# Two of the four weight sums of each group made by accumulating DMAs

## Chip, core and metric

One core of one Trainium2 chip. The metric is device time in microseconds (us) of one launch; a few runs are taken and their median counts. The hardware profiler also records one execution, and every row below is from that one.

## What is computed

The reference is one layer of a hybrid model for 512 prompt tokens and 8 decoded tokens (T = 520 columns). The change lies in its last three products, which are 2048 wide on the input side:

```python
def _channel_and_ple(h, mix, p_l, w_out, g_ffn, w_up, w_down, w_ple, w_ple_norm, w_ple_gate):
    h = h + mix @ w_out
    u = _rmsnorm(h, g_ffn)
    h = h + jnp.square(jax.nn.relu(u @ w_up)) @ w_down
    e = _rmsnorm(p_l @ w_ple, w_ple_norm) * jax.nn.sigmoid(h @ w_ple_gate)
    return h + e
```

## The kernel before

The products with `w_up`, `w_down` and `w_ple_gate` run in 72 groups `g` (32, 32 and 8). One group makes 256 output rows for all 520 columns out of a 2048 x 256 piece of the weights. The group uses a two-by-two scheme with seven products instead of eight (Strassen's scheme in Winograd's form): the piece is cut into four blocks W11, W12, W21, W22 of 1024 x 128, the activations into four as well, and four sums of weight blocks (T1 to T4) and four of activation blocks enter the seven products. In this text the seven products are numbered 0 to 6, their weights being W11, T2, W21, T3, T1, T4 and W22.

A weight is used in two parts of reduced width, high and low: ScalarE (ACT) writes the high part (`w_high`, line 1145, tile `wh`), VectorE (DVE) subtracts it from the weight and writes the low part (`w_low`, line 2460, tile `wl`). TensorE (PE) then does 24 matmuls of 260 columns: 16 with the high weights (lines 1893 and 1895) and 8 with the low ones (line 1900). `wh` and `wl` have two buffers each, so the high part of product n+2 waits for the high matmuls of product n.

The blocks land in six SBUF buffers `rb` of 512 KB each. The sums overwrite blocks that are no longer needed, and a buffer is free for the next load when its last reader is done:

```python
b22 = lambda g: g % 2
b12 = lambda g: 2 + g % 2
b11 = lambda g: 3 - g % 2
B_T, B21 = 4, 5
```

All four sums are DVE instructions: T3 = W22 - W12 into buffer 4 (`sum_t3`, line 2439), T1 = W12 - W11 over W12 (`sum_t1`, line 2444), T2 = W11 + T3 over W11 (`sum_t2`, line 2449) and T4 = W21 - T2 over W21 (`sum_t4`, line 2454). T4 of group g stands on DVE behind the low part of product 2, T3 of group g+1 behind the low part of product 4, T1 of g+1 behind that of product 6, T2 of g+1 behind that of the next group's product 0. The order on each engine is written out by hand: `vector_group` (DVE) and `act_group` (ACT) walk through the seven steps `i` of a group, and the low or high part made in step i is that of product i+1. SyncE (SP) issues nearly all DMAs from one queue in program order and waits before each for its buffer: `block12(g+1)`, `block11(g+1)`, `block21(g+1)`, then the store of hidden rows (in the first 32 groups), then `block22(g+2)`.

Beside this DVE adds the seven products in PSUM up to the four output blocks (lines 2507, 2632, 2642, 2636, `add_first`, `add_second`), makes the activation sums, and every eight groups in `w_down` the whole set of seven activation operands is changed ("a turn"): SP loads operands of 1040 KB each (line 730, tile `af`), ACT and DVE split them (lines 1198 and 2430). GpSimd (POOL) has next to nothing in groups 0 to 63 and adds squares for the last norm in groups 64 to 71 (lines 1401, 1402).

Of the kernel before, what the change touches and what calls it, by code (L numbers as in the profile page):

```python
# [23 lines left out]
P = 128  # L24
# [75 lines left out]
def build(nc, d, d_out):  # L100
    ctx = ExitStack()
    with ctx:
# [349 lines left out]
        t_sum, T_SUM0 = a_b, 64  # L452
        w_lo, W_LO0 = a_nm, 32
# [3 lines left out]
        r_sq, R_SQ0 = d_v, 5  # L457
# [3 lines left out]
        x_i, X_I0 = e_sc, 8  # L461
# [67 lines left out]
        def _(sp):  # L529
# [189 lines left out]
            def operand(c, i):  # L719
# [10 lines left out]
                sp.dma_start(af[n % 9], o_scr[c, SLOT[i]]).then_inc(op_in[n % 4], 16)  # L730
# [28 lines left out]
            for g in range(GN):  # L759
# [8 lines left out]
                if g + 1 < GN:  # L768
                    block12(g + 1)
# [44 lines left out]
        def _(act):  # L814
# [309 lines left out]
            def w_high(w):  # L1124
# [8 lines left out]
                elif i == 1:  # L1133
                    act.wait_ge(t_sum, T_SUM0 + 4 * g + 3)
                elif i == 2:
                    act.wait_ge(b_in[B21], B_IN0[B21] + 16 * (g + 1))
                elif i == 3:
                    act.wait_ge(t_sum, T_SUM0 + 4 * g + 1)
                elif i == 4:
                    act.wait_ge(t_sum, T_SUM0 + 4 * g + 2)  # L1140
# [52 lines left out]
            def operand_high(phase, i, half):  # L1193
                n = 7 * phase + i
                if half == 0:
                    act.wait_ge(op_in[n % 4], OP_IN0[n % 4] + 16 * landings(n))
# [118 lines left out]
        def _(pool):  # L1315
# [95 lines left out]
            pool.wait_ge(h_fin, H_FIN0 + 8)  # L1411
            step(pool.memset(acc, 0.0))  # L1412
            for j in range(8):
                add_squares(16 + j, 0, None, sqg, acc)
# [554 lines left out]
        def _(dve):  # L1969
# [829 lines left out]
```

## Time and profile before

| | |
|---|---|
| median of 3 runs | 2766.38 us (2764.25 to 6148.04) |
| the profiled execution, its own time | 2768.17 us |
| its span in the trace | 2766.4 us |
| granted TensorE clock, mean | 0.955 |
| PE busy | 2527.4 us (91%) |
| DVE busy | 2032.5 us (73%) |
| ACT busy | 1167.5 us (42%) |
| POOL busy | 516.5 us (19%) |
| first and last high matmul of the 72 groups (line 1893) start at | 1184.6 and 2739.1 us |

The 72 groups are 56% of the span. The part ahead of them (input projection, attention, state space part, output projection) is not touched by the change. In the rows below, a line of a view of waits says who waited for whom, how long in all, how often, and the longest; a line of the timeline has the start, the duration, the engine and the line, and in brackets the idle time ahead of it with its releaser.

### The profile page before, as it was taken

What the parts mean: (1) busy time and instruction counts of PE and PEld (TensorE: products, weight loads), DVE (VectorE), ACT (ScalarE), POOL (GpSimd) and SP (SyncE); (2) the same over time, 40 slices, a digit from 0 to 9 for tenths busy, and PEclk for the clock granted to TensorE, in tenths of its full rate; (3) what the DMA queues carried; (4) which work ended last, traced back from release to release, by engine and by line L of the source; (5) the groups of instructions that cost most, each with busy time, mean ns of one, the idle gap of its engine ahead of it and who ended that gap; (6) DMA issues with size and microseconds to landing.
All of it is one profiled execution on the core that took longest, in us unless ns stands there. A gap on an engine that the chain in (4) does not pass through costs nothing. (4 is left out here: it accounts for less than half of the span.)

```text
span 2766.4 us, 50293 instructions
## 1 busy us (share of the span) xinstructions
PE 2527.4 (91%) x20031; PEld 2395.9 (87%) x20031; DVE 2032.5 (73%) x2475; ACT 1167.5 (42%) x1675; POOL 516.5 (19%) x258
## 2 busy tenths in 40 slices
PE   7999999967785899789999999999989999998897
PEld 7999999942354899779999999999989999898897
DVE  4277877627658522698887888888888888889997
ACT  3111111127653322355665665563444434433543
POOL 0099899500018010310000000000000000000022
PEclk9999999988876999899999999999999999999898
DMA  4388898579922332345655656575665646643343
GB/s 134 89 281 272 272 294 297 169 265 389 354 93 84 124 103 97 123 121 163 176 156 163 176 156 179 176 225 162 195 208 179 224 145 192 199 131 100 93 127 126
DMA packets 487361, 498.71 MB, mean 180 GB/s; under 512 B 17270, under 2 KB 434676, under 8 KB 481847
## 3 DMA queue, kind: packets, MB, share of 16 engines
q1 hardware_dynamic: 464136, 482.48, 54.6%
q10 hardware_dynamic: 22990, 13.01, 1.6%
q8 instruction: 159, 2.61, 0.4%
q14 instruction: 76, 0.61, 0.1%
HBM read 428.83 MB, written 66.70 MB: 179 GB/s over the span
## 5 line engine op out<-in xcount | busy, mean ns | idle before, releaser
L1893 PE MATMUL ps<-ah,wh 128*128 128x260 f32 x4032 | 1001.4, 286 | 57.9 <-DVE xsc L2642 13.8
L1895 PE MATMUL ps<-al,wh 128*128 128x260 f32 x4032 | 995.1, 284 | 0.0
L1893 PEld LDWEIGHTS ps<-ah,wh 128*128 128x128 f32 x4032 | 767.9, 190 | 67.5 <-issue 19.4
L1145 ACT ACTIVATE wh<-rb 128x1024 fp32r<-128x1024 f32 x504 | 532.4, 1059 | 671.7 <-PE ps L1895 454.1
L1895 PEld LDWEIGHTS ps<-al,wh 128*128 128x128 f32 x4032 | 768.5, 191 | 0.1
L2460 DVE TENSOR_TENSOR wl<-rb,wh 128x1024 fp32r<-128x1024 f32 x504 | 619.8, 1230 | 100.4 <-ACT wh L1145 97.8
L1900 PE MATMUL ps<-ah,wl 128*128 128x260 f32 x4032 | 576.2, 285 | 16.3 <-DVE wl L2460 15.8
L1900 PEld LDWEIGHTS ps<-ah,wl 128*128 128x128 f32 x4032 | 525.5, 191 | 19.8 <-DVE wl L2460 19.6
L1468 PE MATMUL ps<-uh,wh 128*128 128x260 f32 x1952 | 517.4, 286 | 18.3 <-DVE wl L1978 14.8
L1470 PE MATMUL ps<-ul,wh 128*128 128x260 f32 x1952 | 513.9, 284 | 0.0
L1978 DVE TENSOR_TENSOR wl<-raw,wh 128x1024 fp32r<-128x1024 f32 (+1 forms) x130 | 215.9, 1662 | 258.2 <-ACT wh L839 257.6
L1473 PE MATMUL ps<-uh,wl 128*128 128x260 f32 x1952 | 394.6, 284 | 0.0
L1468 PEld LDWEIGHTS ps<-uh,wh 128*128 128x128 f32 x1952 | 372.2, 191 | 19.8 <-DVE wl L1978 11.3
L1341 POOL TENSOR_TENSOR kpage<-kpage,qbc 128x1024 f32<-128x1024 f32 x128 | 353.9, 2799 | 164.0 <-DMA kpage<-in_cache_k 163.9
L1470 PEld LDWEIGHTS ps<-ul,wh 128*128 128x128 f32 x1952 | 371.4, 190 | 0.0
L839 ACT ACTIVATE wh<-raw 128x1024 fp32r<-128x1024 f32 (+1 forms) x130 | 134.3, 1035 | 561.4 <-PE ps L1473 504.6
L1473 PEld LDWEIGHTS ps<-uh,wl 128*128 128x128 f32 x1952 | 303.4, 190 | 0.0
L1412 POOL MEMSET acc<- 128x520 f32 x1 | 0.5, 532 | 1373.5 <-DVE hT L2555 1373.5
L2045 DVE TENSOR_REDUCE sc<-kpage 128x16 f32<-128x1024 f32 x128 | 154.1, 1212 | 71.8 <-POOL kpage L1341 71.8
L1568 PE MATMUL ps<-vpage,zpad 128*32 128x512 f32 x512 | 78.4, 740 | 32.3 <-DMA vpage<-in_cache_v 32.2
L2444 DVE TENSOR_TENSOR rb<-rb,rb 128x1024 f32<-128x1024 f32 x72 | 95.4, 1325 | 8.2 <-DMA rb<-in_w_down 7.7
L2439 DVE TENSOR_TENSOR rb<-rb,rb 128x1024 f32<-128x1024 f32 x72 | 88.9, 1235 | 16.9 <-issue 15.5
(403 smaller groups left out, 2232.3 us busy)
## 6 DMA issues: line engine op xcount, KB each, us to landing
kpage<-in_cache_k SPq DMA_DIRECT2D x128, 512.0 KB, 4.9
vpage<-in_cache_v SPq DMA_DIRECT2D x128, 512.0 KB, 5.8
rb<-in_w_up SPq DMA_DIRECT2D x128, 512.0 KB, 4.0
rb<-in_w_down SPq DMA_DIRECT2D x128, 512.0 KB, 4.1
raw<-in_w_in SPq DMA_DIRECT2D x88, 512.0 KB, 4.6
af<-o_scr SPq DMA_DIRECT2D x28, 1040.0 KB, 9.9
raw<-in_w_out SPq DMA_DIRECT2D x32, 512.0 KB, 3.4
rb<-in_w_ple_gate SPq DMA_DIRECT2D x32, 512.0 KB, 4.0
```

Source lines behind the costliest of these rows:

```text
L839: A(wh[:, c % 2, 0:elems], raw[:, c % 2, 0:elems], ACT.Copy).then_inc(hi_ready, 1)
L1145: A(wh3[:, w % 2], w_source(g, i), ACT.Copy).then_inc(w_hi, 1)
L1341: pool.tensor_tensor(kpage[:, s], kpage[:, s], qbc[:, b], ALU.mult).then_inc(s_km, 1)
L1468: mm(ps[:, bank + 2 * m + f, 0:HALF], h_, xh[:, f * HALF:(f + 1) * HALF], start=st, stop=False)
L1470: mm(ps[:, bank + 2 * m + f, 0:HALF], h_, xl[:, f * HALF:(f + 1) * HALF], start=False, stop=False)
L1473: z = mm(ps[:, bank + 2 * m + f, 0:HALF], l_, xh[:, f * HALF:(f + 1) * HALF], start=False, stop=en)
L1893: mm(out, wh3[:, w % 2, k], ah[n][:, k], start=fresh and k == 0, stop=False, skip_group_check=True)
L1895: last = mm(out, wh3[:, w % 2, k], al[n][:, k], start=False, stop=False, skip_group_check=True)
L1900: last = mm(out, wl3[:, w % 2, k], ah[n][:, k], start=False, stop=k == KP - 1, skip_group_check=True)
L1978: tt(wl[:, c % 2, 0:elems], raw[:, c % 2, 0:elems], wh[:, c % 2, 0:elems].bitcast(F32), ALU.subtract).then_inc(lo_ready, 1)
L2045: dve.tensor_reduce(sc[:, pg // PAGES, pg % PAGES, :], kpage[:, pg % 4].rearrange("p (c n) -> p c n", n=DK), AX, ALU.add)\
L2460: tt(wl3[:, w % 2], w_source(w // 7, w % 7), wh3[:, w % 2].bitcast(F32), ALU.subtract).then_inc(w_lo, 1)
```

## The change

T3 and T4 are no longer DVE instructions. GpSimd issues for each a DMA from one `rb` buffer to another that adds what it reads to what lies there. Such a DMA can only add, so signs are turned: T3 = W22 + W12, T1 = W12 + W11, T2 = W11 + T3, T4 = W21 + T2, and the signs come back in the activation sums and in the output sums. For T3 the target buffer 4 must first hold W12, so SP loads that block a second time (`block12_again`). T3 of group 0 stays on DVE. One output add over 520 columns (`add_first`) becomes two over 260, as one now adds and the other subtracts. POOL's adding of squares moves into the same loop as its DMAs. Several semaphores are re-used for others, and the landing semaphores of the operands become five instead of four.

```diff
             def block12(g):
                 if g >= 1:
-                    sp.wait_ge(t_sum, T_SUM0 + 4 * (g - 1) + 4)
+                    sp.wait_ge(t4_acc, 16 * g)
                 block(g, b12(g), 0, 1)
+
+            def block12_again(g):
+                sp.wait_ge(w_lo, W_LO0 + 7 * (g - 1) + 4)
+                sp.dma_start(rb[B_T], w_block(g, 0, 1)).then_inc(bt_in, 16)
...
                 if g + 1 < GN:
+                    block12_again(g + 1)
                     block12(g + 1)
...
                 elif i == 3:
-                    act.wait_ge(t_sum, T_SUM0 + 4 * g + 1)
+                    act.wait_ge(t_sum, T_SUM0 + 1)
+                    if g:
+                        act.wait_ge(t3_acc, 16 * g)
...
                 elif i == 5:
-                    act.wait_ge(t_sum, T_SUM0 + 4 * g + 4)
+                    act.wait_ge(t4_acc, 16 * (g + 1))
...
+            def accumulate_t4(g):
+                pool.wait_ge(t_sum, T2_AT(g))
+                pool.wait_ge(w_lo, W_LO0 + 7 * g + 3)
+                pool.dma_start(rb[B21], rb[b11(g)], accum_op=ALU.add).then_inc(t4_acc, 16)
+
+            def accumulate_t3(g):
+                pool.wait_ge(bt_in, BT_IN0 + 16 * g)
+                pool.wait_ge(b_in[b22(g)], B_IN0[b22(g)] + 16 * (g // 2 + 1))
+                pool.dma_start(rb[B_T], rb[b22(g)], accum_op=ALU.add).then_inc(t3_acc, 16)
+
+            for g in range(GN):
+                accumulate_t4(g)
+                if g + 1 < GN:
+                    accumulate_t3(g + 1)
+                if g == GG:
+                    pool.wait_ge(h_fin, H_FIN0 + 8)
+                    step(pool.memset(acc, 0.0))
+                if g > GG:
+                    add_squares(16 + g - GG - 1, 0, None, sqg, acc)
+            add_squares(23, 0, None, sqg, acc)
...
             def sum_t2(g):
-                dve.wait_ge(t_sum, T_SUM0 + 4 * g + 2)
+                dve.wait_ge(b_in[b11(g)], B_IN0[b11(g)] + 16 * (g + 1))
+                dve.wait_ge(t_sum, T1_AT(g))
+                if g:
+                    dve.wait_ge(t3_acc, 16 * g)
                 dve.wait_ge(w_lo, W_LO0 + 7 * g + 1)
                 tt(rb[b11(g)], rb[b11(g)], rb[B_T], ALU.add).then_inc(t_sum, 1)
-
-            def sum_t4(g):
-                dve.wait_ge(t_sum, T_SUM0 + 4 * g + 3)
-                dve.wait_ge(w_lo, W_LO0 + 7 * g + 3)
-                tt(rb[B21], rb[B21], rb[b11(g)], ALU.subtract).then_inc(t_sum, 1)
...
-                tt(both, both, X2.unsqueeze(1).to_broadcast([P, 2, HALF]), ALU.add).then_inc(d_add, 1)
+                p21, p12 = target(g, "21"), target(g, "12")
+                tt(p21, p21, X2, ALU.add).then_inc(d_add, 1)
+                tt(p12, p12, X2, ALU.subtract).then_inc(d_add, 1)
...
-                    if i == 1:
-                        sum_t4(g)
...
-                        if i == 3:
-                            sum_t3(g + 1)
```

On DVE, one group of `w_up` ran before from the low part of product 2 (source `rb5_205`) to that of product 5 as follows; `rb4_204` is buffer 4, which holds T3, and T4 is written into `rb5_205`. The rows from `st_211` to `st_211` are sums of hidden rows.

```order
L2460 TENSOR_TENSOR wl3_207<-rb5_205,wh3_206 128x1024
L2454 TENSOR_TENSOR rb5_205<-rb5_205,rb3_203 128x1024
L2632 TENSOR_TENSOR xsc_208<-xsc_208,ps 128x260
L2460 TENSOR_TENSOR wl3_207<-rb4_204,wh3_206 128x1024
L2526 TENSOR_TENSOR st_211<-sta_212 128x260
L2527 TENSOR_TENSOR st_211<-sta_212 128x260
L2529 TENSOR_TENSOR st_211<-st_211,sta_212 128x260
L2532 TENSOR_TENSOR st_211<-sta_212,st_211 128x260
L2460 TENSOR_TENSOR wl3_207<-rb2_202,wh3_206 128x1024
L2439 TENSOR_TENSOR rb4_204<-rb1_201,rb3_203 128x1024
L2642 TENSOR_TENSOR xsc_208<-xsc_208,ps 128x260
L2460 TENSOR_TENSOR wl3_207<-rb5_205,wh3_206 128x1024
```

The same place on DVE in the changed kernel:

```order
L2484 TENSOR_TENSOR wl3_207<-rb5_205,wh3_206 128x1024
L2661 TENSOR_TENSOR xsc_208<-xsc_208,ps 128x260
L2484 TENSOR_TENSOR wl3_207<-rb4_204,wh3_206 128x1024
L2553 TENSOR_TENSOR st_211<-sta_212 128x260
L2554 TENSOR_TENSOR st_211<-sta_212 128x260
L2556 TENSOR_TENSOR st_211<-st_211,sta_212 128x260
L2559 TENSOR_TENSOR st_211<-sta_212,st_211 128x260
L2484 TENSOR_TENSOR wl3_207<-rb2_202,wh3_206 128x1024
L2671 TENSOR_TENSOR xsc_208<-xsc_208,ps 128x260
L2484 TENSOR_TENSOR wl3_207<-rb5_205,wh3_206 128x1024
```

The two sums (the second row and the tenth of before) are gone, and nothing has taken their place.

On SP's queue, one round of loads before, in the groups of `w_up`; `biased` is the semaphore that the weight sums count on, `neg_max` the one of the low parts.

```order
L678 DMA rb2_202<-in_w_up 128x8x128 [waits biased]
L678 DMA rb3_203<-in_w_up 128x8x128 [waits neg_max]
L678 DMA rb5_205<-in_w_up 128x8x128 [waits neg_max]
L736 DMA o_scr<-st_211 128x7x260 [waits x_rows_decayed]
L678 DMA rb1_201<-in_w_up 128x8x128 [waits neg_max]
```

The same round in the changed kernel:

```order
L694 DMA rb4_204<-in_w_up 128x8x128 [waits neg_max]
L680 DMA rb2_202<-in_w_up 128x8x128 [waits t4_accumulated]
L680 DMA rb3_203<-in_w_up 128x8x128 [waits neg_max]
L680 DMA rb5_205<-in_w_up 128x8x128 [waits neg_max]
L742 DMA o_scr<-st_211 128x7x260 [waits x_rows_decayed]
L680 DMA rb1_201<-in_w_up 128x8x128 [waits neg_max]
```

A load into buffer 4 stands ahead of W12's, and W12's now waits for the landing of GpSimd's DMA; W11, W21, the hidden rows and the next W22 stand behind it in the same queue.

## Rows read from the trace of the kernel before

**Rows 1.** The 72 groups: us, busy PE, PEld, DVE, ACT, POOL, clock, DMA share, GB/s

```profile
1184.00:2741.00 1557.00, 1487.61 (x12111) 1474.45 (x12112) 1331.92 (x1515) 779.05 (x1076) 28.08 (x17) 0.98 0.55 164
```

**Rows 2.** Whom PE waited for from 1184 to 2740 us

```profile
PE ps L1900 <- DVE wl L2460: 15.8, 11, 4.8
PE ps L1893 <- DVE xsc L2642: 13.8, 10, 2.6
PE ps L1893 <- DVE al L2563: 11.0, 2, 8.4
PE ps L1893 <- ACT wh L1145: 10.7, 9, 2.7
PE ps L1893 <- DVE al L2430: 9.4, 9, 2.4
PE ps L1893 <- DVEq L2483: 5.4, 1, 5.4
PE ps L1893 <- issue: 4.5, 8, 0.9
PE ps L1893 <- DVE dt L2507: 2.6, 1, 2.6
```

**Rows 3.** Busy time, same columns: group 12, a turn, the last groups

```profile
1442.00:1462.10 20.10, 20.10 (x170) 20.10 (x170) 16.43 (x21) 15.23 (x32) 0.00 (x0) 1.00 0.54 151
...
2026.00:2055.70 29.70, 22.11 (x168) 20.70 (x169) 29.33 (x33) 16.07 (x18) 0.00 (x0) 1.00 0.56 178
...
2610.00:2740.00 130.00, 123.34 (x1017) 122.03 (x1016) 115.78 (x112) 58.94 (x78) 21.18 (x13) 1.00 0.39 116
```

**Rows 4.** Timeline of DVE in group 12 (products 2 and 3, T4, T3, T1, T2)

```profile
1445.26 1.23 DVE L2460 TENSOR_TENSOR wl<-rb,wh 128x1024 fp32r<-128x1024 f32 x1 [0.23 <-ACT wh L1145]
1446.59 1.23 DVE L2454 TENSOR_TENSOR rb<-rb,rb 128x1024 f32<-128x1024 f32 x1
...
1448.35 1.22 DVE L2460 TENSOR_TENSOR wl<-rb,wh 128x1024 fp32r<-128x1024 f32 x1
...
1452.57 1.22 DVE L2439 TENSOR_TENSOR rb<-rb,rb 128x1024 f32<-128x1024 f32 x1
...
1458.32 1.22 DVE L2444 TENSOR_TENSOR rb<-rb,rb 128x1024 f32<-128x1024 f32 x1
...
1461.18 1.23 DVE L2449 TENSOR_TENSOR rb<-rb,rb 128x1024 f32<-128x1024 f32 x1
```

**Rows 5.** Timeline of ACT: high part of product 5, and of group 13's product 1

```profile
1452.79 1.06 ACT L1145 ACTIVATE wh<-rb 128x1024 fp32r<-128x1024 f32 x1 [0.60 <-PE ps L1895]
...
1462.52 1.06 ACT L1145 ACTIVATE wh<-rb 128x1024 fp32r<-128x1024 f32 x1 [1.67 <-DVE rb L2449]
```

**Rows 6.** PE's line 1893 from 1464.5 us: group 13's product 1 begins

```profile
L1893 PE MATMUL ps<-ah,wh x4: 281/282/288, 1465.1 to 1465.8; 128*128 128x260 f32 x4
```

**Rows 7.** DMA issues of the whole run: KB each, median us to landing

```profile
rb<-in_w_down SPq DMA_DIRECT2D x128, 512.0 KB, 4.1
...
af<-o_scr SPq DMA_DIRECT2D x28, 1040.0 KB, 9.9
...
d_scr<-dt SPq DMA_DIRECT2D x24, 520.0 KB, 2.9
```

**Rows 8.** DMA queue of SP: packets, MB, share of 16 engines

```profile
q1 hardware_dynamic: 464136, 482.48, 54.6%
```

**Rows 9.** Busy time and DMA share ahead of a turn

```profile
2020.00:2025.00 5.00, 5.00 (x42) 5.00 (x43) 2.95 (x5) 0.14 (x2) 0.00 (x0) 1.00 1.05 380
```

**Rows 10.** Timeline of DVE there: T1 of group 40

```profile
2024.91 1.23 DVE L2444 TENSOR_TENSOR rb<-rb,rb 128x1024 f32<-128x1024 f32 x1 [1.91 <-DMA rb<-in_w_down]
```

**Rows 11.** Timeline of DVE in the last groups

```profile
2666.90 1.23 DVE L2439 TENSOR_TENSOR rb<-rb,rb 128x1024 f32<-128x1024 f32 x1 [0.58 <-issue]
...
2672.14 2.34 DVE L2444 TENSOR_TENSOR rb<-rb,rb 128x1024 f32<-128x1024 f32 x1
```

**Rows 12.** ACT's own DMA queue in group 14

```profile
1481.67 5.03 ACTq L1170 DMA_DIRECT2D out_ssm_sample<-stm  x1
```

More of the change, by code:

```diff
@@ L2464, in _ @@
             dve.wait_ge(s_hg, KT)
-            tt(af[place_of(0, 4)], HG["21"], HG["22"], ALU.add).then_inc(u_s, 1)
+            tt(af[place_of(0, 4)], HG["21"], HG["22"], ALU.subtract).then_inc(u_s, 1)
             dve.wait_ge(u_s, U_S0 + 1)
@@ L2506, in finish @@
                 out = target(g, name)
-                tt(out, out if GD <= g < GG else base, bank(g, n), ALU.add).then_inc(ev, 1)
+                if GD <= g < GG:
+                    tt(out, out, bank(g, n), ALU.add).then_inc(ev, 1)
+                else:
+                    tt(out, bank(g, n), base, ALU.add if name == "21" else ALU.subtract).then_inc(ev, 1)
             def read12(g):
@@ L2525, in hidden_sums @@
                     dve.wait_ge(o_out[(g - 1) % 2], stored(g - 1))
-                tt(st[:, SLOT[4]], c21, c22, ALU.add).then_inc(o_sum, 1)
+                tt(st[:, SLOT[4]], c21, c22, ALU.subtract).then_inc(o_sum, 1)
                 tt(st[:, SLOT[3]], c11, c21, ALU.subtract).then_inc(o_sum, 1)
@@ L2531, in hidden_sums @@
                 dve.wait_ge(o_sum, O_SUM0 + 4 * g + 3)
-                tt(st[:, SLOT[6]], c12, st[:, SLOT[1]], ALU.subtract).then_inc(o_sum, 1)
+                tt(st[:, SLOT[6]], c12, st[:, SLOT[1]], ALU.add).then_inc(o_sum, 1)
             def down_start(g):
@@ L2548, in add_second @@
                 dve.wait_ge(ev, EV0 + 5 * g + 2)
-                tt(part, part, U3, ALU.add).then_inc(d_add, 1)
+                tt(part, part, U3, ALU.subtract).then_inc(d_add, 1)
             def h_complete(g):
@@ L2570, in gate_pair7 @@
                 dve.wait_ge(wl_used, WL_USED0 + 7 * GG)
-                tt(n4, p7["21"], p7["22"], ALU.add).then_inc(q_t, 1)
+                tt(n4, p7["21"], p7["22"], ALU.subtract).then_inc(q_t, 1)
                 tt(n3, p7["11"], p7["21"], ALU.subtract).then_inc(q_t, 1)
@@ L2575, in gate_pair7 @@
                 dve.wait_ge(q_t, Q_T0 + 3)
-                tt(n6, p7["12"], n1, ALU.subtract).then_inc(q_t, 1)
+                tt(n6, p7["12"], n1, ALU.add).then_inc(q_t, 1)
             P_ = {k: v[:, 0:7] for k, v in HT_.items()}
@@ L2583, in gate_s2 @@
                 dve.wait_ge(wl_used, WL_USED0 + 7 * (GG - 1) + 2)
-                tt(G1, P_["21"], P_["22"], ALU.add).then_inc(q_p, 1)
+                tt(G1, P_["21"], P_["22"], ALU.subtract).then_inc(q_p, 1)
                 dve.wait_ge(q_p, Q_P0 + 1)
@@ L2593, in gate_s1 @@
                 dve.wait_ge(wl_used, WL_USED0 + 7 * (GG - 1) + 5)
-                tt(G4, P_["21"], P_["22"], ALU.add).then_inc(q_s, 1)
+                tt(G4, P_["21"], P_["22"], ALU.subtract).then_inc(q_s, 1)
             def gate_s4():
@@ L2694, in vector_group @@
                             dve.wait_ge(h_a, 17)
-                            tt(af[6], HG["12"], ah[1].bitcast(F32), ALU.subtract).then_inc(p_s, 1)
+                            tt(af[6], HG["12"], ah[1].bitcast(F32), ALU.add).then_inc(p_s, 1)
                             a_low(0, 5, 0, HG["22"])
```

72 lines of the change are left out of this document (35 added, 37 removed).

## The prediction

> **What bounds the kernel now.** I read the busy time of the 72 groups first. PE is busy 1487.6 of 1557 us and DVE 1331.9 [rows 1], so PE is the bound and DVE close behind. That is a mean over unlike groups. In an ordinary group PE has no gap at all: in group 12 it is busy 20.10 of 20.10 us, DVE only 16.43 [rows 3]. A DVE instruction taken out there is worth nothing. In a turn it is the other way round: DVE is busy 29.33 of 29.70 us and PE 22.11 [rows 3]. In the last groups both are nearly full, PE 123.34 and DVE 115.78 of 130 us [rows 3].
>
> The view of PE's waits gives the ceiling. All of them sum to 15.8 + 13.8 + 11.0 + 10.7 + 9.4 + 5.4 + 4.5 + 2.6 = 73.2 us in the whole stage [rows 2], and no freeing of DVE can give back more. That is 2.6% of 2766; a measurement of this kernel can tell a change of about 2% (55 us) from none.
>
> **What is removed.** 71 T3 and 72 T4, each 1.22 us on DVE [rows 4], about 174 us of busy time. What it is worth has to be read stage by stage.
>
> Last groups (64 to 71): PE lacks 130 - 123.34 = 6.7 us [rows 3]. T3 there even waits 0.58 us for its block, and T1 takes 2.34 us instead of 1.22 while POOL adds squares [rows 11, 4]. Two sums and that wait are 3.0 us of each group's DVE time. The gap is less than 1 us per group on the mean, so it should close: **6.7 us**. The Trainium skill ("SBUF — State Buffer", section "Who interferes with whom") says that a DVE instruction with two SBUF inputs and a GpSimd one that reads SBUF shut each other out; the 2.34 us agree with it. The adding of squares stays in the new kernel, so this changes no term.
>
> Turns (four): DVE is the bound, and two sums, 2.4 us, leave each. **9.8 us** before what the DMAs take back (below).
>
> The first group and the change to the gate (groups 63 and 64) are bound by DVE splitting operands as well: PE's waits 11.0 (line 2563) and 5.4 us [rows 2] are such. One T4 and one T3 leave group 0, and two of each leave groups 63 and 64: 3 x 2.4 = **7.3 us**.
>
> What is left of the 73.2 us lies in scattered groups with an extra DVE instruction (a reciprocal, an operand's low part). I take two thirds of some 6 us: **4 us**. Sum of the gains: 6.7 + 9.8 + 7.3 + 4 = 27.8 us.
>
> The splitting of `add_first` replaces one instruction over 520 columns by two over 260, in 32 groups; both move the same data and DVE has room there. Zero, and 0.1 us per turn if the cover is gone. The turned signs cost nothing, since add and subtract are the same instruction.
>
> **What is added.** 143 DMAs from POOL, 71 more loads of 512 KB, and new waits. POOL is idle in groups 0 to 63, so issuing costs nothing there; in the last groups its squares stand behind the DMAs in program order and feed no one soon. The question is the time L from the accumulating DMA's release to its landing. No row shows such a DMA. The lower end is a plain 520 KB transfer between SBUF and DRAM in a quiet place, 2.9 us. The upper is an operand load of 1040 KB in busy ones, 9.9 us [rows 7]; the accumulate too touches about 1 MB on its reading side, since it must read source and target. A block load of 512 KB takes 4.1 us [rows 7], of which its own time in the rings is small: SP's queue moved 482.48 MB in 54.6% of 2766.4 us, so 0.524 MB takes 1.6 us [rows 8]. Twice that reading plus the same rest, 2 x 1.6 + 2.5, and something for issue by software, makes **L = 6 us**, near the middle. Both ends stay for the range.
>
> The Trainium skill ("DMA: Bandwidth & Descriptors", section "Anatomy of one DMA — SWDGE (gpsimd) path") has 2.0 us plus bytes/436e3 per us for a DMA issued by GpSimd; by that, an estimate, L would be 3.2 us and the slow case below would be out. It is said of plain transfers. The page "SBUF — State Buffer" speaks against this change under "The 'DVE blocks DMA' trap (SWDGE)": GpSimd can't write descriptors while DVE holds the shared port in its two-port modes. Whether DVE's adds count among these no row here can show; if so, a DMA might wait for one more of them, 1.2 us.
>
> Deadlines, from group 12, which starts at about 1442.0:
> - T4: released by product 2's low part, done at 1446.5 [rows 4]. Product 5's high part starts at 1452.79 [rows 5]. Free up to L = 6.3. Product 5 itself begins five sevenths of 20.1 us into the group, at 1456.4, and the high part takes 1.06, so PE waits only from L = 8.8.
> - T3: the new load is released by the low part that ends at 1449.6 [rows 4] and lands 4.1 later, 1453.7. T2 starts at 1461.18 [rows 4], so L = 7.5 is free. The high part that waits for T2 ends at 1463.6 [rows 5] and PE's product 1 begins at 1465.1 [rows 6], 1.5 us of slack: PE waits from L = 9.0.
> - SP's queue: W12's load waited for T4 at 1447.8 before, and now for 1446.5 + L. It lands at 1450.6 + L, and W11's behind it 1.6 later. T1 needs both at 1458.3 [rows 4]: free up to L = 6.1, and with the slack of 1.5 us PE waits from L = 7.6. This is the tightest. Queued behind are W21, the hidden rows and W22.
>
> So with L = 6 an ordinary group still costs 20.1 us.
>
> **DMA traffic** rises. The share is 0.54 in group 12 and 0.56 in a turn [rows 3]. Each group adds a load (1.6 us of ring time) and two accumulates (at least 1.6, at most 3.2 each): 4.8 to 8.0 us of 20.1, to 0.78 to 0.94. Ahead of a turn the rings are full already, share 1.05 [rows 9], and T1 of group 40 waits 1.91 us for its blocks [rows 10]; with W12 held for L more, T1 comes later. Bounds: nothing, or the added 8 us of ring time; I take 1.5 us per turn, as the rings are unused in part while W12 is held, **-6 us**. In eight of the `w_up` groups ACT issues state transfers of its own, and once a full queue held ACT 5.03 us [rows 12]. I take half a microsecond in each: **-4 us**.
>
> Sum: 27.8 - 6 - 4 = 17.8, rounded 18 us. Profiled execution 2768.2 - 18 = 2750.2; it stands 1.8 us above the median, so the **median is 2748 us**.
>
> **Rivals.**
> 1. *The accumulate is long* (slower). If L is above 7.6, each of some 70 groups waits, W11's late landing first. At L = 8.4 that is 0.8 x 70 = 56 us, the 2% line. At 9.9 it is 2.3 x 70 = 161 us: 2927 us. For it: the row of 9.9 us for about as many bytes, software issue, and a DMA share that nears 0.9. Against it: twice the bytes of a 4.1 us load cost only 1.6 us more. Chance 0.24.
> 2. *Crowded DMAs eat the gain*. L lies between 7 and 8.4, or the turns lose 5 us each instead of 1.5 and the state groups 2 us instead of 0.5: 18 - 14 - 12 = -8, so 2774 us, and up to 2815 with some waits in each group. For it: shares of 0.96 and more ahead of turns. Chance 0.25.
> 3. *The whole of the freed DVE time reaches PE*: all the 73.2 us less the clock's and ACT's part (10.7 and 4.5), 58 us: 2708 us. Against it: in the turns DVE still has the splitting to do, of which 2.4 us is a twelfth. Chance 0.03.
> 4. *The change does not do what it says*, PE being the bound in ordinary groups and the DMAs hidden, with no gain in the special ones either: 2766 us. It would need T1 and T2 to wait as long as T3 and T4 took. Part of rival 2, which gives the same sign.
>
> My forecast, 2733 to 2760 us, has 0.48.
>
> **How the numbers follow.** The likeliest case gives 2748 us. Its own range is 2733 (no price for the DMAs and all scattered waits gone) to 2760. The range that holds the time 8 times in 10 must reach into the rivals: from 2728, leaving out rival 3, to 2845, which takes in rival 2 and the milder half of rival 1 (L up to 8.7), and leaves the rest, some 0.15. Faster by over 2% (below 2711): 0.03. Slower by over 2% (above 2822): 0.24. Within: 0.73.
>
> **What would show it.** In the changed profile: an ordinary group at 20.1 us with DVE's busy time near 14 us; landings of the POOL DMAs near 6 us; the last groups at 20.1 us; PE's wait for operands (line 2563 before) smaller by 2 to 5 us. I am wrong if PE waits for ACT's high part, released by a DMA on `rb`, in ordinary groups; if DVE's T1 waits for `rb` from the weights; or if ACT's issues of state DMAs grow long. Most would be off if L is not what I take.

## The result and the profile after

| | before | after |
|---|---|---|
| median | 2765.32 us (4 runs) | 2909.93 us (2899.81 to 2920.83, 4 runs) |
| the profiled execution, its own time | 2768.17 us | 2920.83 us |
| its span | 2766.4 us | 2919.1 us |
| granted TensorE clock, mean | 0.955 | 0.945 |
| DVE busy | 2032.5 us | 1866.0 us |

The ratio is 1.0521, 95% interval 1.0498 to 1.0544. The change makes the kernel 5.2% slower. The ratio and its interval leave out one slow execution of before, at 6148.04 us; the median in the table is over all four. My forecast was 2748 us, with 8 chances in 10 between 2728 and 2845 us; the kernel takes 65 us more than the upper end.

The page of the changed kernel: busy time of the engines, the DMA queues, the chain that ended last and the issues of DMAs.

```profile
PE 2560.3 (88%) x20031; PEld 2419.8 (83%) x20031; DVE 1866.0 (64%) x2364; ACT 1162.6 (40%) x1675; POOL 634.3 (22%) x401
...
q1 hardware_dynamic: 537976, 519.71, 56.5%
q0 software_dynamic: 20592, 74.98, 14.5%
...
PE 33%; DMA 32%; DVE 16%; issue 7%; POOL 6%; ACT 4%; SPq 2%; ACTq 1%; DVEq 0%; POOLq 0%
...
rb<-in_w_down SPq DMA_DIRECT2D x160, 512.0 KB, 5.7
rb<-in_w_up SPq DMA_DIRECT2D x159, 512.0 KB, 5.5
...
rb<-rb POOLq DMA_DIRECT2D x143, 512.0 KB, 6.9
...
rb<-in_w_ple_gate SPq DMA_DIRECT2D x40, 512.0 KB, 6.5
```

DVE lost the 167 us of work that the change takes from it, and the kernel became slower all the same. Read the rows of the issues against [rows 7]: a block load landed in 4.1 us and now takes 5.7, though its own bytes are the same. The queue rows price an accumulating DMA: 14.5% of 2919.1 us, divided by 143, is 2.96 us of all 16 engines for each 512 KB. A plain load costs 1.6 us [rows 8].

Busy time in windows, same columns as [rows 1] and [rows 3]: the 72 groups, group 12, the turn at groups 39 and 40, groups 63 and 64, and groups 65 to 71 of the changed kernel.

```profile
1184.00:2890.00 1706.00, 1517.79 (x12080) 1495.94 (x12081) 1158.98 (x1402) 773.91 (x1075) 144.70 (x160) 0.96 0.83 215
1462.00:1483.50 21.50, 20.36 (x170) 20.18 (x169) 13.68 (x18) 14.82 (x32) 1.72 (x2) 1.00 0.86 216
2085.70:2146.30 60.60, 46.60 (x336) 45.54 (x337) 42.58 (x50) 24.48 (x26) 3.45 (x4) 0.88 0.83 249
2667.70:2731.50 63.80, 46.82 (x337) 45.21 (x338) 59.42 (x61) 31.14 (x34) 3.99 (x5) 0.89 0.49 116
2731.50:2890.00 158.50, 142.45 (x1154) 140.30 (x1153) 108.72 (x116) 69.38 (x89) 28.04 (x26) 0.99 0.68 167
```

The stage grew from 1557 to 1706 us [rows 1], 149 of the 152.7 us by which the span grew. PE's idle time went from 69.4 to 188.2 us (+118.8) and its busy time from 1487.6 to 1517.8 (+30.2). The number of matmuls is the same; they take longer mainly because the clock that was granted fell from a mean of 0.98 to 0.96 in the stage. Summed from the clock records of the two traces, 44 us of the stage were at 1.2 GHz instead of 2.4 before and 119 us after, 14 and 58 of them in the eight groups at the turns; PE's busy time in these stretches rose by 51 us, and half of that, 25 of the 30.2 us, would not be there at 2.4 GHz. In the turn of the table, at 0.88, the clock fell twice: right behind a wait of PE of 1.8 us, and again within a stop of 7.6 us. It falls in ordinary groups too, as behind the wait of 2.76 us shown below for group 13. So a fifth of the loss (30.2 of 149) is a second price of the waits.

Whom PE, DVE, ACT and SP waited for from 1184 to 2890 us in the changed kernel (in all, times, longest).

```profile
PE ps L1919 <- ACT wh L1154: 110.4, 75, 8.0
PE ps L1919 <- issue: 35.3, 4, 9.6
...
DVE rb L2470 <- DMA rb<-in_w_down: 105.6, 29, 12.2
DVE rb L2478 <- DMA rb<-rb: 51.4, 49, 2.8
DVE rb L2470 <- DMA rb<-in_w_up: 45.2, 30, 4.1
...
SPq L680 <- DMA rb<-rb: 250.1, 71, 7.4
```

Line 1919 is the high matmul and line 1154 the high part. That wait was 10.7 us in all before [rows 2] and is 110.4 now. The second row is one long stop of PE in each of the four turns, ahead of product 0 of the second of the two groups. What the first row waits for in its turn is on DVE: T2 (line 2478) waits for the accumulating DMA of T3. T1 (line 2470) waits for block loads. Put down by product, 65.1 us of PE's waits in the 54 ordinary groups stand ahead of product 1, whose weight is T2, and 11.8 ahead of product 0, whose weight is W11. SP, which waited for DVE's T4 before, now stands 250.1 us for the landing of T4's DMA.

Group 12 shows an ordinary group. Its timeline, DVE, POOL, SP, ACT and PE put together by time:

```profile
1467.58 1.22 DVE L2484 TENSOR_TENSOR wl<-rb,wh 128x1024 fp32r<-128x1024 f32 x1
...
1469.34 0.86 POOL L1424 DMA_DIRECT2D rb<-rb  x1 [13.35 <-DVE wl L2484]
...
1470.95 0.37 SPq L694 DMA_DIRECT2D rb<-in_w_up  x1
...
1474.69 2.80 SPq L680 DMA_DIRECT2D rb<-in_w_up  x3
...
1477.88 0.86 POOL L1429 DMA_DIRECT2D rb<-rb  x1 [7.68 <-DMA rb<-in_w_up]
...
1486.80 1.23 DVE L2478 TENSOR_TENSOR rb<-rb,rb 128x1024 f32<-128x1024 f32 x1 [2.81 <-DMA rb<-rb]
...
1488.14 2.02 ACT L1154 ACTIVATE wh<-rb 128x1024 fp32r<-128x1024 f32 x2 [4.38 <-DVE rb L2478]
...
1489.34 0.43 PE L1919 MATMUL ps<-ah,wh 128*128 128x260 f32 x1 [2.76 <-ACT wh L1154]
```

T4 is released when the low part ends, 1468.8, and has landed when SP moves on, 1474.7: L = 5.9 us. SP then issues three block loads in one go, W12's that waited for it and the two that stood behind. The second load of W12, issued at 1470.95, lands at 1477.88, after 6.9 us. T3's DMA follows at once and lands at 1486.80, 8.9 us later. From T4's landing to T3's, 12.1 us, the rings are full:

```profile
1474.70:1486.80 12.10, 11.88 (x100) 11.67 (x98) 6.01 (x8) 7.01 (x15) 0.86 (x1) 1.00 1.02 277
```

(the same view of windows; the DMA share is the second number from the end). A turn shows the other half: ACT's high part of group 40's product 0, and DVE's T1 of the same group, which waited 1.91 us before [rows 10]:

```profile
2117.29 1.06 ACT L1154 ACTIVATE wh<-rb 128x1024 fp32r<-128x1024 f32 x1 [12.21 <-DMA rb<-in_w_down]
2117.21 1.22 DVE L2470 TENSOR_TENSOR rb<-rb,rb 128x1024 f32<-128x1024 f32 x1 [10.76 <-DMA rb<-in_w_down]
```

Both wait for W11, and PE's stop of 7.6 us ends behind the first. In the four turns W11's load is issued 15.6 to 18.9 us after the start of the first group (10.2 to 10.9 before) and takes 13.1 to 14.6 us to land (7.8 to 10.1 before).

### The profile page after: what moved, and what is told of

It reads as the page before. It is cut to its first block, busy times and chain, and to the rows that moved or that the text cites. A ratio compares the mean times of both kernels' runs of the same rounds, so it can differ in the third digit from the quotient of the medians.

```text
span 2919.1 us, 50459 instructions
## 1 busy us (share of the span) xinstructions
PE 2560.3 (88%) x20031; PEld 2419.8 (83%) x20031; DVE 1866.0 (64%) x2364; ACT 1162.6 (40%) x1675; POOL 634.3 (22%) x401
## 3 DMA queue, kind: packets, MB, share of 16 engines
q0 software_dynamic: 20592, 74.98, 14.5%
## 4 chain that ended last, share of the span: by engine, by line
PE 33%; DMA 32%; DVE 16%; issue 7%; POOL 6%; ACT 4%; SPq 2%; ACTq 1%; DVEq 0%; POOLq 0%
DMA rb<-rb 14%; DMA rb<-in_w_down 6%; DMA rb<-in_w_up 6%; PE ps L1494 5%; PE ps L1496 5%; PE ps L1499 5%; PE ps L1919 5%; PE ps L1926 4%; PE ps L1921 4%; POOL kpage L1350 4%; DVE wl L2484 4%; DVE rb L2478 2%; ACT wh L1154 2%; DMA kpage<-in_cache_k 2%; DMA vpage<-in_cache_v 1%
## 5 line engine op out<-in xcount | busy, mean ns | idle before, releaser
L1919 PE MATMUL ps<-ah,wh 128*128 128x260 f32 x4032 | 1021.5, 290 | 182.8 <-ACT wh L1154 110.4
L1921 PE MATMUL ps<-al,wh 128*128 128x260 f32 x4032 | 1011.3, 287 | 0.0
L1919 PEld LDWEIGHTS ps<-ah,wh 128*128 128x128 f32 x4032 | 779.7, 193 | 201.6 <-issue 161.5
L1154 ACT ACTIVATE wh<-rb 128x1024 fp32r<-128x1024 f32 x504 | 525.6, 1057 | 835.5 <-DVE rb L2478 209.8
L1921 PEld LDWEIGHTS ps<-al,wh 128*128 128x128 f32 x4032 | 781.3, 194 | 0.1
L1494 PEld LDWEIGHTS ps<-uh,wh 128*128 128x128 f32 x1952 | 372.3, 191 | 17.5 <-DVE wl L2004 10.2
L1424 POOL DMA_DIRECT2D rb<-rb x72 | 62.4, 866 | 1026.4 <-DVE wl L2484 935.0
L1429 POOL DMA_DIRECT2D rb<-rb x71 | 61.2, 862 | 515.1 <-DMA rb<-in_w_up 228.2
## 6 DMA issues: line engine op xcount, KB each, us to landing
af<-o_scr SPq DMA_DIRECT2D x28, 1040.0 KB, 10.2
```

Of the source, the lines that this page charges most:

```text
L1154: A(wh3[:, w % 2], w_source(g, i), ACT.Copy).then_inc(w_hi, 1)
L1494: mm(ps[:, bank + 2 * m + f, 0:HALF], h_, xh[:, f * HALF:(f + 1) * HALF], start=st, stop=False)
L1919: mm(out, wh3[:, w % 2, k], ah[n][:, k], start=fresh and k == 0, stop=False, skip_group_check=True)
L1921: last = mm(out, wh3[:, w % 2, k], al[n][:, k], start=False, stop=False, skip_group_check=True)
```

## Experiments

Each run is timed beside runs of the kernel before; the ratio and its 95% interval are to those. The table takes the 72 groups apart. A group's time is the difference between the starts of the first high matmul of its product 0 and of the next group's, read from each trace; for group 71 it ends with the start of its last matmul. "Ordinary" is the mean of the groups without a turn from 1 to 30; "turns" is the sum of the eight groups 31, 32, 39, 40, 47, 48, 55 and 56. The DMA share is the mean of the 72 groups. All columns behind the ratio come from one trace per version, and that of the changed kernel is of the slowest of its four executions, 11 us above their median; so differences of a few us between rows are not shown to be real.

| run | median us | ratio, 95% | all 72 | ordinary | turns | 63 + 64 | mean 65 to 71 | DMA share |
|---|---|---|---|---|---|---|---|---|
| before | 2765.32 | | 1555.5 | 20.45 | 206.1 | 66.4 | 21.32 | 0.55 |
| after | 2909.93 | 1.0521 (1.0498 to 1.0544) | 1707.2 | 22.36 | 244.7 | 63.8 | 23.05 | 0.83 |
| A sums back on DVE | 2768.95 | 1.0008 (0.9994 to 1.0023) | 1561.1 | 20.41 | 208.8 | 66.5 | 21.83 | 0.54 |
| B only T4 by DMA | 2990.02 | 1.08 (1.0778 to 1.0823) | 1784.2 | 23.36 | 239.5 | 66.1 | 25.13 | 0.59 |
| C only T3 by DMA | 2822.44 | 1.0197 (1.0178 to 1.0217) | 1613.5 | 20.89 | 225.0 | 63.1 | 22.69 | 0.75 |
| D copies, nothing added | 2789.14 | 1.0076 (1.0056 to 1.0096) | 1582.4 | 20.60 | 227.3 | 60.9 | 21.14 | 0.76 |
| E no second load | 2837.58 | 1.0264 (1.0246 to 1.0281) | 1623.6 | 21.21 | 231.3 | 61.3 | 22.27 | 0.80 |
| F W12's load later in the queue | 2901.4 | 1.0469 (1.042 to 1.0518) | 1694.0 | 22.33 | 231.9 | 62.7 | 23.00 | 0.84 |
| G as B, T3 later on DVE | 2817.64 | 1.0187 (1.017 to 1.0204) | 1612.4 | 20.64 | 236.7 | 64.2 | 22.67 | 0.66 |
| H G and F together | 2860.62 | 1.0339 (1.032 to 1.0358) | 1656.3 | 21.23 | 228.3 | 62.6 | 23.20 | 0.64 |
| I DVE sums in turn groups | 2881.84 | 1.0412 (1.0396 to 1.0428) | 1673.3 | 22.40 | 217.0 | 62.7 | 22.88 | 0.81 |
| J DMA sums in 11 groups | 2786.6 | 1.0071 (1.0057 to 1.0085) | 1575.4 | 20.40 | 232.5 | 59.4 | 21.59 | 0.60 |
| K DMA sums from group 64 on | 2774.57 | 1.0033 (1.0021 to 1.0045) | 1561.6 | 20.41 | 207.3 | 60.2 | 23.18 | 0.59 |
| L DMA sums in 3 groups | 2760.93 | 0.9987 (0.9977 to 0.9997) | 1551.6 | 20.46 | 206.7 | 60.9 | 21.68 | 0.57 |

The changed kernel's 151.7 us (1707.2 - 1555.5) are some 103 in the 54 ordinary groups (1.91 each), 38.6 in the turns, 12.1 in groups 65 to 71, and -2.5 in groups 0, 63 and 64.

**A. Everything but the DMAs.** Signs, the split output add, semaphores and the place of POOL's squares stay; T4 and T3 are DVE instructions again, at their old places.

```diff
+        BY_DMA4 = lambda g: False
+        BY_DMA3 = lambda g: False
...
+                    if i == 1 and not BY_DMA4(g):
+                        dve_t4(g)
...
+                        if i == 3 and not BY_DMA3(g + 1):
+                            dve_t3(g + 1)
```

> Both sums are back on DVE; the turned signs, the split output add and the re-used semaphores stay, no load is doubled and no DMA accumulates. All theories of the DMAs (crowded rings; latency of two DMAs in a row; loads held in SP's queue) expect the time of before, 2766 us, give or take 8. If the signs or the extra waits on DVE were the cause, it would stay near 2900.

Measured 2768.95 us, no difference from before (0.9994 to 1.0023). The whole loss comes with the DMAs, the second load and their waits. In its trace the last groups are longer than before all the same, 21.83 us against 21.32, and those of J and L, which also have DVE sums in all or nearly all of them, are at 21.59 and 21.68. So a part of what later runs seem to lose in groups 65 to 71 against before may be there without any DMA; one trace each does not settle it.

**B and C. One sum at a time.** The same switches, with `BY_DMA4` true alone in B, `BY_DMA3` true alone in C; B has no second load.

> Only T4 by an accumulating DMA; T3 on DVE, no second load of W12. W12's load still waits for T4's landing. Crowded rings: the added traffic falls from some 7.6 to 3.0 us of ring time per group, share about 0.70, so most of the loss goes: 2760 to 2790 us. Held loads in SP's queue: the loss of the four turns stays (about 9 us each): 2795 to 2820. Latency of the DMA pair load-then-accumulate: that pair is gone, 2760 to 2780.

> Only T3 by a second load and an accumulating DMA; T4 on DVE, so W12's load waits for DVE as before. Crowded rings: 4.7 us of ring time added, share about 0.75, half of the loss or less: 2790 to 2840. Latency of the pair: T2 still waits for it in each group, 1 us or more per group: 2840 to 2890. Held loads: gone, and with it nearly all the loss of the turns: 2860 or less by this alone.

B gave 2990.02 us, worse than both DMAs together, where no theory had more than 2820. The waits of B from 1184 to 2740 us:

```profile
PE ps L1924 <- DVE xsc L2690: 151.8, 61, 8.0
...
DVE rb L2474 <- issue: 238.9, 52, 10.5
```

Line 2474 is T3, on DVE at step 3. W12's load is held in SP's queue until T4 has landed, so T3 cannot start when its turn comes, and DVE, which runs in order, stands there 238.9 us. PE then waits for what lies behind it on DVE, the output sums (line 2690). The new wait is on SP, and the engine that pays is a third one. C has the second load and one accumulate per group and costs 2.0%: of the 58.0 us in the 72 groups 18.9 are in the turns, and some 31 in the ordinary groups. 2822.44 us lies in the range of crowded rings. The loss in the turns, which the theory of held loads had put at nearly nothing here, is half of the changed kernel's.

**D. Copies in place of accumulates.** The same DMAs at the same places, but without adding: T4 becomes a copy of T2 and T3 a copy of W22, so the weights of two products are not the scheme's sums.

```diff
-                pool.dma_start(rb[B21], rb[b11(g)], accum_op=ALU.add).then_inc(t4_acc, 16)
+                pool.dma_start(rb[B21], rb[b11(g)]).then_inc(t4_acc, 16)
...
-                pool.dma_start(rb[B_T], rb[b22(g)], accum_op=ALU.add).then_inc(t3_acc, 16)
+                pool.dma_start(rb[B_T], rb[b22(g)]).then_inc(t3_acc, 16)
```

> The changed kernel with plain copies in place of the two accumulating DMAs (same bytes, buffers, queue and semaphores): T3 and T4 are wrong values, W22 and T2 in place of the sums. A packet of 4 KB took 328 ns accumulating and a plain one of 4160 bytes 161 ns, so each of them should need 1.5 us less of the rings. Crowded rings: share from 0.90 to about 0.75, time 2790 to 2850. Latency or queue order as such: little changes, 2880 to 2910.

The queue and issue rows of D's page:

```profile
q0 software_dynamic: 20592, 74.98, 7.1%
...
rb<-in_w_down SPq DMA_DIRECT2D x160, 512.0 KB, 5.3
...
rb<-rb POOLq DMA_DIRECT2D x143, 512.0 KB, 4.7
```

Packets and bytes are those of the changed kernel, the share is half: 7.1% of 2789.6 us over 143 is 1.4 us of ring time for a copy, against 2.96. The landing falls from 6.9 to 4.7 us, and the time by 121 us, to 2789.14. Issue by GpSimd, the second load, the waits and the order all stay in D, so these together cost 21 us (a ratio of 1.0076 on 2767.94), though GpSimd writes a copy faster (0.53 us of issue against 0.86), and the adding itself brings the rest. The time is a little under the range that crowded rings had. The landings by line, T4's and then T3's, of the changed kernel and then of D:

```profile
DMA to landing us min/median/max: 4.5/5.5/9.6
DMA to landing us min/median/max: 5.3/7.8/12.3
...
DMA to landing us min/median/max: 2.8/3.4/8.4
DMA to landing us min/median/max: 3.5/5.9/11.6
```

An adding DMA lands some 2 us later than a copy, the quickest ones as well (4.5 and 2.8 us), and packet by packet the trace has 328 ns for 4096 bytes added and 160 ns for 4096 copied (medians; 327 and 156 at the least). So D shortens the path of each sum and empties the rings at once, and no run separates the two. In the 72 groups D still loses 26.9 us, 21.2 of them in the turns.

**E. No second load.** T3's DMA adds W22 to whatever lies in buffer 4, so T3 is not the scheme's sum; the load and its wait are gone.

```diff
-                    block12_again(g + 1)
...
-                pool.wait_ge(bt_in, BT_IN0 + 16 * g)
+                pool.wait_ge(w_lo, W_LO0 + 7 * (g - 1) + 4)
```

> The changed kernel without the second load of W12: T3's DMA adds W22 to whatever lies in buffer 4, so T3 is a wrong value. It is released by the low part of product 3, as the load was, some 7 us earlier than now. The chain load-then-accumulate is gone and 1.7 us of ring time per group; 5.9 us of added ring time and the held loads stay. Chain theory: ordinary groups fall from 22.3 to 20.3-20.6 us, 2790 to 2815 us in all. If it is the rings being crowded by the accumulates alone: 2840 or more.

E takes 2837.58 us, between the theories and close to that of the crowd. The issue rows of its page:

```profile
rb<-rb POOLq DMA_DIRECT2D x143, 512.0 KB, 5.8
rb<-in_w_up SPq DMA_DIRECT2D x128, 512.0 KB, 5.7
```

72 us are won by taking out 1.6 us of ring time and one link of the chain, but a plain load still takes 5.7 us (6.7 in the groups of `w_down`). Ordinary groups fall to 21.21 us, a little over half of the way to the 20.3 to 20.6 that the chain theory had. The crowd stays without the second load; the chain is shorter. Halving the ring time of GpSimd's DMAs (D, -121) is worth more than removing a whole load and its link (E, -72).

**F. Another order in SP's queue.** W12's first load stands behind W11's, so the wait for T4 no longer holds operands 3 and 4 and W11.

```diff
                     block12_again(g + 1)
-                    block12(g + 1)
...
                     block11(g + 1)
+                    block12(g + 1)
```

> The changed kernel with W12's load, which waits for T4's landing, moved behind the operands 3 and 4 and W11's load in SP's queue. Held-loads theory: the four turns lose 20 to 30 us less (244.7 us for their eight groups now), ordinary groups stay at 22.3, since T2 waits for T3's chain: 2880 to 2890 us. Crowding alone: nothing changes, 2900 to 2915.

F takes 2901.4 us, which is in the range that I had given to crowding alone, and its interval overlaps that of the changed kernel. In the trace the turns fall from 244.7 to 231.9 us and the ordinary groups stay at 22.3. So the place in the queue costs at most some 13 us, in the turns, where I had expected 20 to 30. W11 is issued 10.2 to 12.7 us into the turn again, nearly as early as before, but still takes 13.2 to 14.5 us to land: the crowd, and not only the holding, delays it.

**G and H. T4 by DMA with T3 out of its way.** As B, with DVE's T3 two steps later (`i == 5` in place of `i == 3`); H also has F's order.

> T4 by an accumulating DMA, T3 on DVE as in the run with T4 alone (2990 us), but T3 stands two steps later on DVE, right ahead of T1. If that run was slow because DVE stood at T3 in its order waiting for W12, whose load waits for T4's landing, ordinary groups fall from 23.5 to 20.3-20.6 us, and the whole to 2775-2800 us, turns still slower than before. If it was the accumulating DMA itself, it stays above 2900.

> The same with W12's load moved behind the operands 3 and 4 and W11's load in SP's queue, as in the run that moves only that. Held loads: the turns come back to about 206 us for the eight groups, 2755 to 2775 us in all; DVE has one sum less per group, worth up to 15 us in turns and last groups. If crowding by 3 us of ring time per group matters: 2775 to 2800.

G is 172 us faster than B from that one move, which shows that most of B's loss was DVE standing at T3. At 2817.64 us it is still 18 us above the range that I gave, by the turns. Its issue rows:

```profile
rb<-in_w_up SPq DMA_DIRECT2D x88, 512.0 KB, 5.0
rb<-rb POOLq DMA_DIRECT2D x23, 512.0 KB, 4.6
```

(from 1300 to 1760 us). T4's accumulate, alone in its group and in rings with a share of 0.75 in this window (0.66 over the 72 groups), lands in 4.6 us, and the ordinary groups are within 0.2 us of before up to group 30 and within 0.6 later (20.87 against 20.30). It still loses 1.9%, 30.6 us of it in the turns. H missed: I expected F's order to bring the turns back to about 206 us, and they only fall from 236.7 to 228.3; and the loads of W12 come later for DVE's T3 in the ordinary groups, which rise from 20.64 to 21.23:

```profile
PE ps L1925 <- ACT wh L1159: 63.8, 55, 4.8
...
DVE rb L2475 <- issue: 46.0, 26, 3.5
```

(waits of H from 1184 to 2740 us; line 2475 is T3, line 1159 the high part).

**I and J. Where the turns lose.** In I the eight turn groups have DVE sums and all others DMA sums; J is the reverse, with groups 0, 63 and 64 added to the eight.

```diff
+        BY_DMA4 = lambda g: g not in (31, 32, 39, 40, 47, 48, 55, 56)
+        BY_DMA3 = lambda g: g - 1 not in (31, 32, 39, 40, 47, 48, 55, 56)
```

> Both sums by DMA everywhere except in the eight groups at the four turns (31, 32, 39, 40, 47, 48, 55, 56), where DVE makes T4 and the next group's T3 and no block is loaded twice. In the changed kernel these eight groups take 244.7 us together, 38.6 more than before (206.1). Theory 'the crowd at the turn itself': the extra load, the two accumulates and the order that holds W12's load meet the operand loads, so with the DVE sums these groups go back to 206 to 215 us, the ordinary groups stay at 22.3, and the time is 2875 to 2885. Rival 'inherited': the loads come late into the turn because the groups before it have already filled the queue, then the turns stay above 230 us and the time above 2895.

> The reverse: both sums by DMA only where VectorE is the bound or nearly so (groups 0, 31, 32, 39, 40, 47, 48, 55, 56, 63 and 64), everywhere else as in the kernel before. This is the place from which the prediction drew 9.8 + 7.3 us of gain. Theory 'the crowd at the turn itself': the eight turn groups take 235 to 245 us, ordinary groups 20.3, and the time is 2790 to 2805. Rival 'inherited': the turns are at 200 to 206 us, since nothing before them has filled the rings, groups 63 and 64 save 2.6, and the time is 2750 to 2762, faster than before.

I came out as the first theory had it, 2881.84 us, with the turns at 217.0, 2 us above its range. J is close to it too: 2786.6 us and turns of 232.5, a little under what it gave, and far from the rival's gain. Groups 39 and 40 in a window each, of before, of I and of J:

```profile
2004.50:2055.70 51.20, 42.68 (x338) 40.84 (x337) 44.12 (x50) 24.70 (x26) 0.00 (x0) 1.00 0.70 236
```

```profile
2078.90:2131.50 52.60, 42.69 (x338) 40.86 (x337) 44.86 (x52) 24.61 (x26) 0.00 (x0) 1.00 0.70 234
```

```profile
2008.00:2065.60 57.60, 43.59 (x338) 42.37 (x337) 39.66 (x48) 24.56 (x26) 3.45 (x4) 0.91 0.88 261
```

With crowded neighbours but its own sums on DVE the turn costs 1.4 us more than before; with quiet neighbours and its own sums by DMA, 6.4. In J DVE has 4.5 us less to do there and PE is idle 14.0 us instead of 8.5. In the changed kernel it is 60.60 us: idle 14.0, and busy 46.6 instead of 42.7, the clock. Of the 38.6 us of the four turns, 27.7 go when the turn itself is given back (I) and 11 stay, which I put down to the groups around, though A's turns are 2.7 us above those of before without any DMA.

**K. DMA sums from group 64 on**, where the DMA share was 0.39 [rows 3].

```diff
+        BY_DMA4 = lambda g: g >= GG
+        BY_DMA3 = lambda g: g >= GG
```

> Both sums by DMA only from group 64 on, where the rings are least busy (share 0.39 before) and TensorE had a gap of under 1 us per group. Theory 'ring time alone decides': with a share of at most 0.39 + 6.5 / 21 = 0.70 the landings are quick and the gap closes, 2758 to 2764. Rival 'order decides': the last groups take about 23.0 us as in the changed kernel (21.3 before), since the chain of reload, accumulate and T2 is as long as the time it has even in a quieter ring, and the time is 2775 to 2782.

K takes 2774.57 us, nearer to the rival. Groups 63 and 64 save 6.2 us, and groups 65 to 71 give back 13 (23.18 instead of 21.32 each), 9.5 if A's 21.83 is the measure. Busy time and issues of K from 2610 to 2750 us:

```profile
2610.00:2750.00 140.00, 122.90 (x999) 120.54 (x1000) 95.57 (x103) 59.23 (x78) 26.00 (x23) 1.00 0.66 163
```

```profile
rb<-in_w_ple_gate SPq DMA_DIRECT2D x24, 512.0 KB, 6.4
rb<-rb POOLq DMA_DIRECT2D x11, 512.0 KB, 5.7
```

PE has the work of [rows 3]'s last row in 10 us more, and DVE 20 us less work. A mean share of 0.66 still gives landings of 6.4 us, where they were 4.0 in before. The mean hides bursts; one that SP's queue makes is in K's timeline, four loads issued within 5.42 us when T4 has landed:

```profile
2667.41 5.42 SPq L695 DMA_DIRECT2D rb<-in_w_ple_gate  x4
```

and in K's windows the 10 us behind it are full, share 1.02, and the next 10 nearly empty, 0.37:

```profile
2670.00:2680.00 10.00, 7.81 (x64) 7.41 (x62) 6.18 (x7) 2.86 (x4) 2.99 (x3) 1.00 1.02 270
2680.00:2690.00 10.00, 8.50 (x71) 8.54 (x72) 7.79 (x9) 5.21 (x7) 0.87 (x1) 1.00 0.37 68
```

**L. Only groups 0, 63 and 64.**

```diff
+        BY_DMA4 = lambda g: g in (0, 63, 64)
+        BY_DMA3 = lambda g: g - 1 in (0, 63, 64)
```

> Both sums by DMA in three groups alone: 0, 63 and 64, where VectorE splits operands and the rings have room. In the run with eleven such groups these three took 91.7 us against 99.7 before, while the turns lost 26.4. Theory 'gain where VectorE is the bound and the rings are not': 6 to 8 us less than before, 2759 to 2761, a ratio of about 0.9975. Rival 'nothing is left of it', since the gain is given back in the next groups or lies within what runs differ by: 2765 to 2768.

2760.93 us over 12 runs against 2765.7, ratio 0.9987 (0.9977 to 0.9997): the only version faster than the kernel before, by 4.8 us and not the 6 to 8 expected; the interval only just leaves out 1. The three groups take 93.3 us instead of 99.7. Groups 65 to 71 take 2.5 us more than before in all, but less than A's, so this need not be a price of the DMAs. Groups 63 and 64 of L, then of before:

```profile
2519.30:2580.20 60.90, 46.82 (x338) 45.39 (x337) 57.64 (x59) 31.12 (x34) 3.99 (x5) 0.86 0.50 118
```

```profile
2524.50:2590.90 66.40, 48.54 (x338) 47.11 (x338) 62.56 (x62) 31.37 (x34) 0.53 (x1) 0.85 0.24 70
```

Here DVE is the bound (62.56 of 66.40 us) and the rings are at 0.24. Its busy time falls by 4.9 us and the time by 5.5. This is the case in which the idea works.

## Why the prediction was wrong

**The step that failed** is what I put into the deadline of T3, the times from issue to landing: "the new load is released by the low part that ends at 1449.6 [rows 4] and lands 4.1 later, 1453.7", with one L = 6 for every accumulate behind it. The traffic term of the same text had the share of group 12 at 0.78 to 0.94, and it came out as 0.86; but the 4.1 us were taken from a kernel with 0.55 in the stage. With the budget as I had made it, from the release of the second load PE has 4.1 + 9.0 = 13.1 us. In group 12 of the changed kernel the chain took 1486.80 - 1470.95 = 15.9 us (6.9 for the load, 8.9 for the accumulate). The difference is 2.8 us, and PE waits 2.76. The deadlines were right; the landings were those of another kernel. Group 12 is one of many: over the 54 ordinary groups the chain takes 14.1 us on the mean and more than 13.1 in 42 of them, and in D, where it takes 10.7, in 2. An ordinary group is 1.91 us longer than before, 1.4 of it idle time of PE and 0.5 busy time at the lower clock. D and E support it by two different cuts: with copies the ordinary group is at 20.60, with the link removed at 21.21.

**L itself.** "L = 6 us, near the middle": T4 in group 12 took 5.9, and the median of T4 is 5.5 us from issue to landing in the changed kernel and 4.6 in G. T3's took 8.9, past the 7.5 that I called free, with a median of 7.8, and 6.7 in C, where it is the only accumulate. L is not a constant but depends on what is issued beside it: T3's DMA shares the rings with the three loads that T4's landing has just let go. The ring time was bounded well, 1.6 to 3.2 us, with 2.96 measured, near the upper end. The Trainium skill ("DMA: Bandwidth & Descriptors", section "Anatomy of one DMA — SWDGE (gpsimd) path") would give 3.2 us by its formula, an estimate. The plain copies that D has in the place of T4 come near it, with a median of 3.4 us and 2.8 at the least, but not those in the crowded place of T3 (5.9). No accumulate does: the quickest took 4.5 us.

**The queue of SP** was called the tightest deadline, "free up to L = 6.1". In group 12, with T4 at 5.9, T1 waited 0.89 us all the same, as the loads behind T4 landed late too, and nobody waited for T1. In the turns it failed: T4 of group 39 took 9.1 us from issue to landing, and W11 came late for PE itself.

**The turns** were priced at 1.5 us each for traffic, against a gain of 2.4. They cost 9.6 each (38.6 / 4). The bound that I gave was "the added 8 us of ring time"; taking a fifth of it "as the rings are unused in part while W12 is held" was the mistake, since what is held is also W11 and two operands, and all of it comes in one burst on rings that had a share of 1.05 at that point [rows 9]. F prices the holding at 13 us at most, and I shows 28 us to be made in the turn groups themselves. These effects overlap (C, which holds nothing, still loses 19 in the turns, G, which loads nothing twice, 31), and I cannot split them cleanly. The halved clock behind the long waits was in no term.

**Gains.** "3 x 2.4 = 7.3 us" for groups 0, 63 and 64: right in mechanism and size where the rest is left as it was, 6.4 in L and 8.0 in J (32.3 + 59.4 against 99.7); in the changed kernel only 2.5 is left. "6.7 us" for the last groups: wrong in sign, +12.1 in groups 65 to 71 (the row that I took for 64 to 71 begins at the end of group 65). K shows that the DMA sums do most of this: its groups 65 to 71 take 9.5 us more than A's. DVE has the work less, and the chain of load, accumulate and T2 puts a longer gap in its place. Signs and the split add: nothing in the whole time, as forecast (A). The term of 4 us for ACT's state transfers was too small: the issue in group 14 that took 5.03 us before [rows 12] takes 9.10, and that one group is 30.3 us long instead of 24.6.

```profile
1508.82 9.10 ACTq L1179 DMA_DIRECT2D out_ssm_sample<-stm  x1
```

The 4 us for scattered groups were not measured apart. Of the signs of being wrong that I had named, all three came: PE waiting for high parts behind a DMA on `rb`, T1 waiting for weights, and this issue.

**The trap of the shared port.** The prediction left open whether DVE's adds hold up GpSimd's writing of descriptors. In group 12 the DMA is issued 0.54 us after its release (1468.80 to 1469.34), and POOL's issue takes 0.86 us with DVE adding and subtracting beside it; 0.86 is the shortest and the median of the 72 issues of T4, so nothing of the kind is seen. The Trainium skill ("SBUF — State Buffer", section "Who interferes with whom") says that an instruction of two tensors has no two-port mode, so it is not one of those that the trap is about; the trace agrees.

**The rivals.** The result came by rival 1's wait (W12 and T3 too late for T2, PE waiting in each ordinary group), caused by rival 2's mechanism (landings lengthened by the DMAs' own traffic). I had treated them as separate, the one set by a fixed L and worth 2927 us at L = 9.9, the other by turns and state groups and capped at 2815. That they feed each other, that more traffic makes L long, was the missing thought. That rival 1's 2927 us lies near the 2910 measured is in part luck: T4's L stayed under its 7.6 in ordinary groups (median 5.4), W11's late landing holds PE for 11.8 us in the ordinary groups where T2's holds it for 65.1, and a quarter of the loss is in the turns, which rival 1 leaves out. With 0.24 on it the chance of slower by over 2% was too small, since its condition was argued from a transfer in quiet rings.

No run isolates why an adding DMA stays twice as long in the rings as a copy of the same packets and bytes. D shows that it does, and that the adding makes most of the loss; how much of that is the DMA's own later landing and how much the delay of the others stays open.

## What to carry to other kernels

When a change adds transfers to rings that are more than half full, work out the new share first and take every landing on the path, old ones too, from rows at that share; a median of the kernel before is the landing of another kernel. Moving work from a fast engine to DMA paid here only in the groups where that engine is the bound and the rings are nearly empty (L, 5 us), and cost in the turns, the ordinary groups and the last groups, even where the mean share had looked harmless. A wait put into an in-order queue is paid by whatever stands behind it and by whoever waits for that: hold a load back only when nothing urgent is queued behind, and look for the burst when it is let go.

## What the runs showed of the hardware

- An accumulating DMA between SBUF buffers took 2.96 us of the rings for 512 KB, a plain one by the same queue 1.4 us (14.5% and 7.1% of the span for 143 of each). The median packet of 4096 bytes took 328 ns and 160 ns.
- It landed in a median of 4.6 us as T4 alone (G, share 0.66 over the 72 groups), 6.7 us as T3 alone with a further load (C, 0.75), and 5.5 and 7.8 us as T4 and T3 with both (0.83). The quickest took 4.5 us, and the quickest copy 2.8.
- GpSimd needed 0.86 us to issue an accumulating DMA and 0.53 us (mean of 143) for the copy of the same tiles.
- In a turn where PE waited 1.8 us and later stood still for 7.6, the granted clock went to 1.2 GHz behind the first and during the second; its mean in the window was 0.88 instead of 1.00, and the same matmuls took 46.6 us instead of 42.7.
